# Sparse attention's inputs and the recurrence's output projection on products of rounded parts

## The reference, cut to what matters

```python
y = _rwkv7_time_mix(hin, ...)            # ends with: return out @ w_out, v_first
x = _layernorm(DEEPNORM_ALPHA * x + (1 + gt1) * y, ...)
...
# _dsa_attention(h, ...)
proj = h @ w_in                          # queries 1024, latent 128, index queries 512, index key 64, index weights 8
ckv = _rmsnorm(proj[..., c1:c2], kv_norm)
s = jnp.einsum('bthd,bsd->bths', qib, k_idx)
score = jnp.einsum('bth,bths->bts', wib, jax.nn.relu(s))
_, idx = lax.top_k(score, k_sel)         # the 128 best keys of each query
```

## Time and profile before

| | |
|---|---|
| median of 3 runs | 2845.82 us (2843.67 to 2848.26) |
| the profiled execution | 2844.33 us, span 2842.5 us |
| mean granted TensorE clock | 0.978 of full |
| busy share of the span | PE 95%, PE weight loads 71%, DVE 48%, ACT 37%, POOL 12% |
| DMA | 261 MB, mean 92 GB/s |

### The profile page before, as it was taken

The page is one execution under the profiler, slowest core; times in us unless marked ns, Lnnn a source line. Parts: engine busy times, 40 slices in busy tenths (PEclk is TensorE's granted clock), DMA queues, the critical chain, the costliest instruction groups (busy, mean ns, idle before and its releaser), DMA issues.

```text
span 2842.5 us, 46206 instructions
## 1 busy us (share of the span) xinstructions
PE 2707.7 (95%) x19024; PEld 2007.3 (71%) x19024; DVE 1369.2 (48%) x2302; ACT 1038.4 (37%) x1598; POOL 343.4 (12%) x268
## 2 busy tenths in 40 slices
PE   7999998899999989989999989999889999999999
PEld 4566666468888644577888868888677667788886
DVE  6566656253333337754333354433447676344335
ACT  5334333144432231744442243232223574333223
POOL 3232323010000101401000020000013131000000
PEclk9999999889999999999999989999989999999999
DMA  5344433322232112022223212232231002222231
GB/s 227 104 132 134 139 126 110 108 82 103 90 119 89 63 45 74 1 89 74 103 89 117 91 45 103 89 120 84 82 112 67 2 9 97 89 89 103 102 113 59
DMA packets 46585, 261.12 MB, mean 92 GB/s; under 512 B 5161, under 2 KB 7609, under 8 KB 26201
## 3 DMA queue, kind: packets, MB, share of 16 engines
q1 hardware_dynamic: 45416, 254.23, 25.8%
q10 hardware_dynamic: 1008, 4.57, 0.4%
HBM read 256.63 MB, written 2.15 MB: 91 GB/s over the span
## 4 chain that ended last, share of the span: by engine, by line
PE 89%; DVE 4%; ACT 3%; POOL 1%; issue 1%; DMA 1%; SPq 0%; DVEq 0%; ACTq 0%; POOLq 0%; PEld 0%; PEldq 0%
PE psum L220 87%; PE psum L2081 2%; DMA ada_first<-in_ada_first 1%; POOL ysum L568 0%; POOL branch_in L570 0%; DVE residual L1545 0%; ACT L614 0%; POOL join L563 0%; DVE weights L254 0%; DVE residual L1537 0%; ACT yg L648 0%; ACT ln_in L1500 0%; ACT nsa_probs L2117 0%; DVE Y_pairs L776 0%; DVE ln_stat L1529 0%
## 5 line engine op out<-in xcount | busy, mean ns | idle before, releaser
L220 PE MATMUL psum<-ffn_in_hi,ffn_weights_hi 128*128 128x512 f32 x848 | 339.9, 401 | 20.7 <-DVE ffn_in_lo L1652 8.4
L220 PE MATMUL psum<-ffn_in_lo,ffn_weights_hi 128*128 128x512 f32 x848 | 333.9, 394 | 0.0
L220 PE MATMUL psum<-ffn_in_hi,ffn_weights_lo 128*128 128x512 f32 x848 | 333.5, 393 | 0.0
L1674 ACT ACTIVATE ffn_weights_hi<-weights 128x1024 fp32r<-128x1024 f32 (+1 forms) x128 | 145.9, 1142 | 490.5 <-PE psum L220 490.5
L1674 ACT ACTIVATE ff_weights_hi<-weights 128x1024 fp32r<-128x1024 f32 (+1 forms) x120 | 137.7, 1147 | 433.3 <-PE psum L220 433.3
L220 PE MATMUL psum<-ff_in_hi,ff_weights_hi 128*128 128x512 f32 x704 | 277.5, 394 | 11.7 <-DVE ff_in_lo L1551 7.2
L1677 DVE TENSOR_TENSOR ff_weights_lo<-weights,ff_weights_hi 128x1024 fp32r<-128x1024 f32 (+1 forms) x116 | 156.0, 1345 | 253.8 <-ACT ff_weights_hi L1674 253.8
L220 PE MATMUL psum<-ff_in_lo,ff_weights_hi 128*128 128x512 f32 x704 | 276.2, 392 | 0.0
L220 PE MATMUL psum<-ff_in_hi,ff_weights_lo 128*128 128x512 f32 x704 | 276.1, 392 | 0.0
L1677 DVE TENSOR_TENSOR ffn_weights_lo<-weights,ffn_weights_hi 128x1024 fp32r<-128x1024 f32 (+1 forms) x126 | 166.9, 1327 | 110.5 <-ACT ffn_weights_hi L1674 110.5
L220 PEld LDWEIGHTS psum<-ffn_in_hi,ffn_weights_hi 128*128 128x128 f32 x848 | 161.7, 191 | 61.1 <-DVE ffn_weights_lo L1677 9.2
(11 more groups left out here) (560 smaller groups left out, 4865.3 us busy)
## 6 DMA issues: line engine op xcount, KB each, us to landing
weights<-in_ff_in SPq DMA_DIRECT2D x44, 1024.0 KB, 4.8
weights<-in_ffn_in SPq DMA_DIRECT2D x44, 1024.0 KB, 4.8
weights<-in_ada SPq DMA_DIRECT2D x80, 512.0 KB, 3.8
weights<-in_ff_out SPq DMA_DIRECT2D x16, 1408.0 KB, 6.0
weights<-in_ffn_out SPq DMA_DIRECT2D x16, 1408.0 KB, 6.1
weights<-in_rwkv SPq DMA_DIRECT2D x8, 1152.0 KB, 5.5
weights<-in_rwkv SPq DMA_DIRECT2D x8, 640.0 KB, 4.0
weights<-in_ada_first SPq DMA_DIRECT2D x4, 1024.0 KB, 11.4
```

The source lines that it names most:

```text
L220: return nc.tensor.matmul(out, lhsT, rhs, start=start, stop=stop)
L1674: return nc.scalar.activation(sp_.hi[u][:, 0:width], slot[s][:, u * width:(u + 1) * width], ACT.Copy)
```

## The change

In the recurrence's output projection:

- `project` is gone. The projection is now `split_project` with half tiles of four 128x128 blocks. Its input is split by `recurrence_parts`: ACT first rounds half of the first weight tile, then the eight input tiles, with the second half of the weights after two of them; DVE makes the rests. `by_tile` makes PE wait for each input tile of the first output tile by itself.
- The residual is fetched in four DMAs of 512 KB from ACT's queue, issued after the second input tile is rounded, and POOL scales each quarter. DVE waits for quarter j/2 ahead of the weight split that it makes at output tile j.

In the sparse attention:

- "ln01" now writes `h` as parts (into the buffer of the attention's output, free until then) and also keeps it whole, because its buffer is used as scratch later. Its `units` are the first index weights: ACT rounds those of latent and keys (four instructions of 512 columns) behind the last square, and index tiles 0 and 1 and the small weights behind the standard deviation; POOL makes the rests.
- Latent, index keys and all four index tiles are three passes each. For input tiles 0 to 3 PE does latent and keys, then index tiles 0 and 1, then for tiles 4 to 7 all four together.
- The index weights come from 24 passes with 8 weight columns and 512 moving columns, a copy by ACT and four small products that turn them.
- The bias rows use another bank, and PE's wait for DVE's latent moves behind the scores.
- The index queries are not padded: a step makes two 64-row products (two heads) into two banks, and one relu takes both. There are 12 steps for 24 and as many additions. POOL no longer clears the buffer.
- The eight queries are three passes each; ACT rounds their weights, POOL makes the rests, in buffers under the attention's probabilities. SP issues their loads between the bias windows. On PE queries 0 and 1 come ahead of the flips, the others behind them.

Semaphores of the gated and projecting layers are shared between layers (`steps_again` with turns). The diff, cut:

```diff
-        def steps_again(name, names):
+        def steps_again(name, names, turns=1):
...
-            in_turn[name] = s, base + 2 * len(names)
+            in_turn[name] = s, base + (turns + 1) * len(names)
...
-        def project(name, stream, sources, ready, factor, x_ready=()):
...
+        def residual_again(ready):
...
+                for q in range(4):
+                    act.dma_start(x[:, 2 * q:2 * q + 2, :], d["x"][:, 2 * q:2 * q + 2, :]).then_inc(x_in[q], 16)
...
+                    nc.gpsimd.tensor_scalar(x[:, 2 * q:2 * q + 2, :], x[:, 2 * q:2 * q + 2, :], ALPHA, None, ALU.mult).then_inc(
+                        *pool_done.step(f"scaled{q}"))
...
+        def recurrence_parts(y, parts, halves, ready, fetch):
...
+                act.wait_ge(*reached(*ready))
+                halves.first_hi(act, 0)
+                for k in range(KT):
+                    if k == 2:
+                        halves.first_hi(act, 1)
+                    nc.scalar.activation(parts[0][:, k, :], y[:, k, :], ACT.Copy).then_inc(*act_done.step(f"hi{k}"))
+                    if k == 1:
+                        fetch(act)
...
+                halves.first_lo(dve, 0)
+                for k in range(KT):
+                    if k == 4:
+                        halves.first_lo(dve, 1)
+                    dve.wait_ge(*act_done(f"hi{k}"))
+                    nc.vector.tensor_tensor(parts[1][:, k, :], y[:, k, :], parts[0][:, k, :].bitcast(F32), ALU.subtract).then_inc(
+                        *dve_done.step(f"lo{k}"))
...
                 for j in range(KT):
                     i, s = j // 2, j % 2
+                    if by_tile and j % 2 == 0:
+                        dve.wait_ge(*reached(*x_ready[j // 2]))
...
             def pe(pe):
...
+                for k in range(4):
+                    pe.wait_ge(*reached(*branch[k]))
+                    for bank, name in enumerate(("ckv", "kidx")):
+                        if k == 0:
+                            pe.wait_ge(*lo_split(name))
+                        step(name, bank, k)
+                for bank, name in ((2, "qi0"), (3, "qi1")):
+                    pe.wait_ge(*lo_split(name))
+                    for k in range(4):
+                        step(name, bank, k)
+                for k in range(4, KT):
+                    pe.wait_ge(*reached(*branch[k]))
+                    for bank, name in ((0, "ckv"), (1, "kidx"), (2, "qi0"), (3, "qi1")):
+                        step(name, bank, k)
...
+                    for hh in range(2):
+                        r = slice(hh * HD, (hh + 1) * HD)
+                        last = mm(ps[:, SCORES[t % 2][hh], 0:w], qi[r, m % 2, q * P:(q + 1) * P], kidx[r, 0:w])
+                    last.then_inc(*pe_done.step(f"score{t}"))
+                pe.wait_ge(*dve_done("ckv"))
...
+                def query(j):
+                    n, i = j % 2, j // 2
+                    pe.wait_ge(*q_lo(f"lo{n}", i))
+                    pe.wait_ge(*q_act(f"query{n}", i, 1))
+                    for k in range(KT):
+                        w = slice(k * P, (k + 1) * P)
+                        last = three_of(ps[:, n, :], (held[2 * n][:, w], held[2 * n + 1][:, w]), (h[0][:, k, :], h[1][:, k, :]), k == 0, k == KT - 1)
+                    last.then_inc(*q_pe.step(f"query{n}"))
...
             def act(act):
...
+                act.wait_ge(*load_c.arrived())
+                for n in (2, 3):
+                    nc.scalar.activation(held[n], of_slot(slot, f"qi{n}"), ACT.Copy).then_inc(*act_done.step(f"hi qi{n}"))
...
+                    if t == 5:
+                        query_hi(0)
+                query_hi(1)
...
+                def query(j):
...
+                    nc.scalar.activation(qs[:, j, :], ps[:, n, :], ACT.Copy, scale=-HD ** -0.5).then_inc(*q_act.step(f"query{n}"))
+                    if j + 2 < KT:
+                        query_hi(j + 2)
...
             def pool(pool):
...
+                q_lo.enter(pool)
+                for j in range(KT):
+                    pool.wait_ge(*q_hi(f"hi{j % 2}", j // 2))
+                    nc.gpsimd.tensor_tensor(held[2 * (j % 2) + 1], query_raw(j), held[2 * (j % 2)].bitcast(F32), ALU.subtract).then_inc(
+                        *q_lo.step(f"lo{j % 2}"))
```

More of the change, by code:

```diff
@@ L1451, in layer_norm, with made @@
+        def layer_norm(name, scope, layer, half_layer, sums, following, units=None, whole=None):
             parts = following and isinstance(following[3], tuple)
             gain, into, rooted = (following[1], following[4], following[5]) if following and following[0] == "gain" else (None, None, None)
-            full = keep(f"{name}_in", [P, 2, T], scope) if parts else None
+            full = keep(f"{name}_in", [P, 2, T], scope) if parts and whole is None else None
+            def made(j):
+                return whole[j] if whole else full[:, j % 2, :]
@@ L1497, in act @@
                     to = following[3]
[L1498 removed]
+                    if parts and j >= 2 and whole is None:
                         act.wait_ge(*dve_done(f"lo{j - 2}"))
[L1500 removed]
+                    nc.scalar.activation(made(j) if parts else to[:, j, :], x[:, j, :], ACT.Identity, bias=shift[:, j:j + 1],
                                          scale=vcol(gain, j) if gain else mod(following[0], following[2], j)).then_inc(*act_done.step(f"in{j}"))
@@ L2226, in sparse_attention @@
             scratch = d["bias_scratch"]
-            todo = [(m, hh, q) for m in range(IH // 2) for hh in range(2) for q in range(1, QT)]
+            todo = [(m, q) for m in range(IH // 2) for q in range(1, QT)]
             NI = len(todo)
-            pe_done = steps("idx_pe", ["ckv", "kidx", "widx", "qi0", "qi1", "ckv sq", "bias"]
-                         + [n for t, (m, hh, q) in enumerate(todo)
-                            for n in (([f"qi{m + 1}"] if hh == 0 and q == 1 and m >= 1 and m < 3 else []) + [f"score{t}"])])
@@ L2232, in sparse_attention @@
-            act_done = steps("idx_act", ["ckv sq", "kidx", "qi0a", "qi0b", "ckv std", "far", "bias"]
-                          + [n for t, (m, hh, q) in enumerate(todo)
-                             for n in ([f"relu{t}"] + ([f"qi{m + 1}a", f"qi{m + 1}b"] if hh == 0 and q == 3 and m < 3 else []))])
-            dve_done = steps("idx_dve", ["widx", "ckv rstd", "ckv"] + [f"add{t}" for t in range(NI)] + [f"causal{q}" for q in range(1, QT)])
+            SCORES = ((6, 7), (4, 5))
+            pe_done = steps("idx_pe", ["ckv", "kidx", "qi0", "qi1", "ckv sq", "widx", "bias", "widx turned"]
+                         + [n for t, (m, q) in enumerate(todo) for n in [f"qi{m + 1}"] * (q == 1 and 1 <= m < 3) + [f"score{t}"]])
@@ L2236, in sparse_attention @@
+            act_done = steps("idx_act", ["ckv sq", "kidx", "qi0", "qi1", "ckv std", "widx", "far", "bias", "hi qi2", "hi qi3"]
+                          + [n for t, (m, q) in enumerate(todo) for n in [f"relu{t}"] + [f"qi{m + 1}"] * (q == 1 and 1 <= m < 3)])
+            dve_done = steps("idx_dve", ["ckv rstd", "ckv", "widx"] + [f"add{t}{hh}" for t in range(NI) for hh in range(2)]
+                             + [f"causal{q}" for q in range(1, QT)])
             topk_done = steps("top_dve", [f"max{q}" for q in range(1, QT)] + [f"take{q}" for q in range(1, QT)])
```

408 lines of the change are left out of this document (216 added, 192 removed).

## The result

The changed kernel took 2800.89 us, the median of four runs (2796.28 to 2807.38), beside 2847.04 (2843.67 to 2850.36) for the kernel before: ratio 0.9838, 95% interval 0.9824 to 0.9853. Five more runs later gave 0.9826 (0.9812 to 0.9839). The prediction was 2798 with 2789 to 2817. The profiled execution took 2798.2 us with a span of 2796.4, 46.1 less than before.

A forecast was written before the change was run, and what follows sets the result against it. PE was taken to bound the kernel, with 89% of the chain. 7.9 us off the recurrence's projection and 40 off the attention, 48 off 2844.3, give 2796.4; the median stands 1.5 above, so 2798, range 2789 to 2817.

The forecast's parts named there:

- The recurrence's projection: Recurrence's output projection: last update at 577.2 instead of 585.1, 7.9 us less, bounds 9.4 to 1.4.
- The stall of 1.5 for the residual: Recurrence's projection: DVE, then PE, waits for the residual's first scaled quarter, 0 to about 2.8 us, middle 1.5.
- Rival 2: Recurrence's projection: residual comes as late as at the kernel's start, stall 8 instead of 1.5, total 2804; chance 0.10.
- The norm: Layer norm ahead of the attention: 12.0 us from last update to first product, 3.3 later; floor 10.75 from the next norm.
- the bound of 15.45: Norm ahead of the attention: top if two more DVE steps are each held by a 2.35 us POOL split.
- Index products: Sparse attention: 96 one-pass products for latent, keys and two index tiles, 21.9 us plus 2.1 for a cold start.
- Top-k's start: Sparse attention, after the scores: DVE's top-k starts at 1036.6 instead of 1060.9.
- The restart at half clock: Sparse attention: 2.1 us given back for one more half-clock start, since PE is sparse from 1009 to 1013.
- Two paths within 1 us: Start of the attention: DVE and POOL's masks and PE's queries and keys arrive within 1 us of each other.
- my 40: Sparse attention as a whole: 40 us less, bounds 20 and 44.
- Rivals 1 and 3: POOL's splits hold the top-k, total 2817, chance 0.12; the top-k starves POOL, about 2870, chance 0.03, milder 2818 to 2840, 0.05.
- Rival 4: More gain: shorter norm behind the recurrence's projection and no cold restart, total 2793; chance 0.10.

The follow-up runs named there:

- the two parts alone: Kernel before with only the recurrence's projection changed: ratio 0.9976; with only the sparse attention changed: ratio 0.9855.
- one_fetch: Changed kernel with the residual fetched in one DMA of 2 MB instead of four of 512 KB: ratio 0.9855 to the kernel before.
- causal_early: Changed kernel with the causal masks subtracted after the first three score steps instead of ahead of the top-k: median 2796.5 us.
- no_residual: Changed kernel without the second fetch of the residual and without its scaling: ratio 0.984 to the kernel before.

## Why the prediction was right, point by point

- **What bounds it.** PE did, and three one-pass products were worth 11 us on 64 products (46.97 us for 57.86). Shown by the two parts alone.
- **The recurrence's projection**, forecast 7.9 less, was 8.8 less. The start of 2.2 us after the recurrence was 2.1. The stall of 1.5 for the residual did not exist as a wait. What is there is contention, and it was missing from this term: 0.7 us where the clock rises early, 0.16 us of PE's gaps in the changed kernel's own profile. I had POOL scale a quarter in 1.5 us "when nothing holds it"; it takes 2.8 with DVE idle (`one_fetch`), and 2.9 and 3.3 beside the remainders. So that price was wrong from the start and not by contention: the fastest of eight rows of another operation was no price for this one. The four landed early enough all the same. ACT also issued the fetches at once (532.73), not after two roundings; its queue runs ahead of its arithmetic. From the first product to the last update it is 46.99 us for the forecast's 46.3 + 1.5: the residual and a later clock together are 0.7. Rival 2 (a late residual, 8 us) is refuted for four fetches; `one_fetch` shows that its mechanism is real and costs 5.
- **The norm**, forecast 12.0 us, was 10.87 and, in the second profile, 13.18. The forecast lies between the two, and which of them comes is set by the moment at which the clock falls (last section), for which this term had no line. The floor of 10.75 was nearly met for another reason than I gave. It held one hold of 1.66 us (L1529 beside a split of 1,024 columns). Here three operations are held, by 0.68, 0.59 and 0.59, together 1.86. The step that failed is that I took each hold at up to 2.35 us: the first units here are split in pieces of 512 columns, 1.25 us each (2.51 for two), so the first two holds are short, and the third meets only the end of a longer split. The Trainium skill, SBUF — State Buffer ("SBUF: two separate sides"), says that such a pair excludes each other for the whole instruction. The trace agrees for the splits: DVE's 1.28 ends 0.54 us behind POOL's half, which ended at 962.51. It does not for POOL's scaling, which held one remainder by 0.84 us and let two pass at full speed within the same instruction. That the bound of 15.45 was too high because the instructions that hold are short is read from these rows; no run put a long split there.
- **Index products**: 24.0 us forecast for 96 with their cold start, 24.7 measured (968.33 to 993.06). The first relu was forecast 47.9 us after the last update and stood at 45.5, as much earlier as the norm and shorter handoffs gave.
- **Top-k's start**, forecast 24.3 us earlier, was 22.5 (74.8 for 97.3), although its lead-in stood 2.4 ahead. Missing from that sum were two holds that I had not looked for past the norm: the second score operation (2.46 us for 0.48) and the causal masks (2.71 for 0.69). Only the second counts: DVE's wait of 3.65 us swallowed the first, and the 2.0 of the masks, made up by their move in `causal_early`, and the restart of 1.5 explain most of the delay. (The sum has a slip of its own: from 1027.1 its listed terms, 7.4 and 1.0, give 1035.5 and not 1036.6.) The restart at half clock, given back with 2.1 at the end of the sum, came in the gap where I had put it, behind the first scores, and cost 1.5.
- **Two paths within 1 us**: keys at 122.0, first mask at 123.6. They meet, but not within 1 us: with the 1.1 that the keys take and the 1.4 of the first masks they are 1.9 apart, DVE's the later one, so the change gives back 2.3 us at the masks that my 40 had no line for; 38.5 came (36.4 in the second profile).
- **Rivals 1 and 3** needed a hold between one-input top-k instructions and POOL's splits. There is none in either direction.
- **Rival 4** (2793) expected the norm behind the recurrence's projection to become shorter. It took 10.76, 12.1 and 11.7 in profiles of this code; no property of the change.

So the mechanism was right, and the two main terms, 8.8 for 7.9 and 38.5 for 40. That the total came so close, 46.1 for 48, is in part luck: prices inside both terms were off in both directions, and stages that the change doesn't touch moved by 4.5 us one way and 5.5 the other, mostly with the clock.

## What to carry to other kernels

Before a split is put on POOL, list every two-input DVE operation within its time, not only in the stage that it was made for, and ask of each hold whether the engine waits anyway soon after; a hold of 2.0 us cost the full 2.0 ahead of the top-k and nothing behind the first scores. In the norm the holds beside POOL's 512-column pieces were 0.6 to 0.7 us and the one beside a 1,024-column split 1.66; that cutting the splits is what made them short is an argument from these rows, not a test. Take the price of an instruction from the same instruction, not from the fastest of another one. When a faster engine brings two paths together, shorten the cheaper-looking one alone and read how little it gives; then you know the gain lies in both. Stages a few us long are compared by offsets from a common event, against a second profile of the same kernel, and with the granted clock of both beside them: twice in this study a difference of 1.5 us that looked like the edit's was the clock's.

## What the runs showed of the hardware

Profiles differ by several us in code that none of the edits touch, and most of that is the granted clock. The windows before the recurrence, 20 to 70 and 70 to 95 us, columns PE, PEld, DVE, ACT, POOL busy, PEclk, DMA share and GB/s, of the kernel before:

```profile
20.00:70.00 50.00, 49.51 (x180) 21.50 (x180) 39.58 (x80) 35.02 (x49) 22.79 (x7) 0.97 0.48 181
...
70.00:95.00 25.00, 20.64 (x98) 10.36 (x100) 11.93 (x17) 8.17 (x14) 6.15 (x4) 0.97 0.23 73
```

and of the changed one:

```profile
20.00:70.00 50.00, 49.81 (x176) 21.66 (x176) 37.04 (x77) 34.49 (x48) 22.79 (x7) 0.90 0.49 184
...
70.00:95.00 25.00, 21.86 (x67) 9.51 (x65) 13.11 (x21) 8.56 (x15) 2.23 (x2) 0.93 0.14 48
```

The clock was 0.90 and 0.93 instead of 0.97, PE's two blocks there took 51.9 and 17.6 us for 49.7 and 15.9 in the chain, which is 3.9 of the 5.5 us by which the recurrence ended later. In the fourteen profiles of this study it ended between 526.0 and 532.7. Only one of them is of the kernel before (527.2), so a small part that belongs to the change can't be excluded.

In the norm it is the moment at which the clock falls. Windows from the last update (us, PE busy, PEclk), first profile of the changed kernel:

```profile
959.50:961.50 2.00, 2.00 (x11) 1.00 0.00 0
...
961.50:963.50 2.00, 0.93 (x3) 1.00 0.00 0
...
965.50:967.50 2.00, 0.00 (x0) 0.58 0.01 4
```

second profile:

```profile
957.60:959.60 2.00, 2.00 (x11) 1.00 0.00 0
...
959.60:961.60 2.00, 1.39 (x3) 0.50 0.00 0
...
963.60:965.60 2.00, 0.00 (x0) 0.50 0.01 4
```

PE did the same in both, full until 4 us after the update and sparse behind that. In one it went on at full clock (2.4 GHz) until about 8 us after, in the other it was at half (1.2 GHz) from 4 us on. A pair of the norm's products then takes up to 2.08 us instead of 1.12, and all that follows is 2.3 us later, as the table under "Which path" shows. A term for a cold start in a sum should therefore be a range, not a number: behind the first scores it was 0, 1.5 and 3.0 us in three kernels with the same PE instructions in that stretch (`no_residual`, the changed kernel, `causal_early`; the fourth relu stood at 53.7, 55.2 and 56.7).
